# Attention by units of two heads, its scaling on GpSimd, weight tiles released before evictions, and Gram products that alternate heads

## What is computed

```
def causal_block_attention(q, k, v, scale):      # 8 heads, q and k 96 wide, v 64 wide
    for blk in range(S // Q_BLOCK):              # 8 blocks of 128 queries
        s = jnp.einsum('bqhd,bkhd->bhqk', qb, k[:, :kend]) * scale
        s = jnp.where(mask, s, -1e30)
        prob = jax.nn.softmax(s, axis=-1)
        outs.append(jnp.einsum('bhqk,bkhd->bqhd', prob, v[:, :kend]))
```

## Time and profile before

| | us |
|---|---|
| median of three runs | 4064.01 (4061.86 to 4067.34) |
| the profiled run | 4065.56 |
| its span | 4064.3 |
| granted TensorE clock, mean | 0.949 of full |
| TensorE busy | 3753.2, 92% of the span |
| VectorE, ScalarE, GpSimd busy | 1815.3, 1317.5, 1172.0 |

### The profile page before, as it was taken

One profiled execution on the slowest core, in us unless ns is written; L12 is line 12 of the kernel. 1 busy time (PEld: TensorE's weight loads), 2 busy tenths in 40 slices (PEclk: granted clock), 3 DMA queues, 4 the chain that ended last, 5 costly groups with the idle time before them and its releaser, 6 DMA issues.

```text
span 4064.3 us, 44734 instructions
## 1 busy us (share of the span) xinstructions
PE 3753.2 (92%) x18398; PEld 3094.9 (76%) x18398; DVE 1815.3 (45%) x2380; ACT 1317.5 (32%) x2129; POOL 1172.0 (29%) x624
## 2 busy tenths in 40 slices
PE   5998998979799987999999898999987989999998
PEld 4786877878777766888888767777666868888886
DVE  3435444444155534233233353887543444444435
ACT  3323132222344323221221343776123233232323
POOL 3322313231100232333333211576133313222321
PEclk8988898988999999999999999999999999999999
DMA  4101010000100343111111222222344421111111
GB/s 119 53 1 53 1 46 19 19 29 18 39 12 1 99 144 95 50 50 47 50 49 47 73 88 86 70 86 86 99 154 143 148 80 50 47 48 51 47 47 52
DMA packets 282074, 253.63 MB, mean 62 GB/s; under 512 B 11333, under 2 KB 221569, under 8 KB 281872
## 3 DMA queue, kind: packets, MB, share of 16 engines
q1 hardware_dynamic: 267264, 216.52, 17.7%
q10 hardware_dynamic: 11520, 25.17, 1.6%
q0 software_dynamic: 3088, 9.10, 0.6%
HBM read 214.04 MB, written 36.70 MB: 62 GB/s over the span
## 4 chain that ended last, share of the span: by engine, by line


## 5 line engine op out<-in xcount | busy, mean ns | idle before, releaser
L401 POOL TENSOR_TENSOR weight_lo<-stage,weight_hi 128x1024 fp32r<-128x1024 f32 (+4 forms) x265 | 634.5, 2400 | 1551.9 <-ACT weight_hi L393 1551.7
L364 PE MATMUL psum<-hT_hi,weight_hi 128*128 128x512 f32 x2240 | 895.8, 400 | 13.7 <-ACT sig_g L744 6.6
L365 PE MATMUL psum<-hT_lo,weight_hi 128*128 128x512 f32 x2240 | 882.0, 394 | 0.0
L366 PE MATMUL psum<-hT_hi,weight_lo 128*128 128x512 f32 x2240 | 881.3, 393 | 0.0
L364 PEld LDWEIGHTS psum<-hT_hi,weight_hi 128*128 128x128 f32 x2240 | 427.9, 191 | 112.3 <-issue 16.0
L365 PEld LDWEIGHTS psum<-hT_lo,weight_hi 128*128 128x128 f32 x2240 | 427.2, 191 | 93.8 <-issue 6.1
L366 PEld LDWEIGHTS psum<-hT_hi,weight_lo 128*128 128x128 f32 x2240 | 426.3, 190 | 89.8
L393 ACT ACTIVATE weight_hi<-stage 128x1024 fp32r<-128x1024 f32 (+4 forms) x329 | 313.5, 974 | 462.2 <-PE psum L366 381.7
L1935 DVE TENSOR_TENSOR x<-x,psum 128x512 f32<-128x512 f32 x432 | 290.1, 686 | 216.4 <-PE psum L366 215.8
L364 PE MATMUL psum<-weight_hi,act_hi 128*128 128x512 f32 x864 | 339.9, 393 | 0.0
L366 PE MATMUL psum<-weight_hi,act_lo 128*128 128x512 f32 x864 | 339.4, 393 | 0.0
(11 more groups left out here) (371 smaller groups left out, 6045.9 us busy)
## 6 DMA issues: line engine op xcount, KB each, us to landing
stage<-in_w_in SPq DMA_DIRECT2D x64, 512.0 KB, 4.0
stage<-in_w_up SPq DMA_DIRECT2D x44, 512.0 KB, 3.9
scratch_gates<-gate ACTq DMA_DIRECT2D x64, 256.0 KB, 2.0
gs<-scratch_gates SPq DMA_DIRECT2D x64, 256.0 KB, 2.8
stage<-in_w_out SPq DMA_DIRECT2D x32, 512.0 KB, 4.8
stage<-in_w_ffn_up SPq DMA_DIRECT2D x32, 512.0 KB, 4.0
stage<-in_w_ffn_down SPq DMA_DIRECT2D x32, 512.0 KB, 3.9
stage<-in_w_down SPq DMA_DIRECT2D x22, 512.0 KB, 3.4
```

Of the source, the lines that this page charges most:

```text
L364: q.matmul(out, stat[0], mov[0], start=first, stop=False)
L365: q.matmul(out, stat[0], mov[1], start=False, stop=False)
L366: return q.matmul(out, stat[1], mov[0], start=False, stop=final)
L401: g.q.tensor_tensor(lo, K.staged(w), hi.bitcast(F32), ALU.subtract).then_inc(*S.w_lo_pool.up(w))
```

## The change

**Attention.** A unit is a block of queries of both heads of a pair: 32 units, a lag of one unit between steps where it was two for the transposes. The scores of head h use banks 2h and 2h+1 (2h alone for narrow units); P and PT have four buffers each, two heads of two units. After a unit's two exponents VectorE takes both reciprocals (`dve_exponent`), and GpSimd multiplies each P in place by them (`pool_exponent`, 64 instructions, widths 128 to 1024); only then does TensorE transpose. Three banks, 4 to 6, take the transposes and the fed steps. The output product has `vh` stationary (64 columns) and PT moving (128 columns), the two heads in turn to partitions 0 to 63 and 64 to 127 of bank 7, so that the result is oT itself: ScalarE writes oT_hi (32 of 128x128, L1617), VectorE oT_lo. `otok`, its 64 evictions, 32 transposes and 16 evictions go. The next pair's steps are fed two at a time, from the third of a pair's eight iterations.

**Releases.** In the merges, the compression and the feed-forward's last group, `released` stands between TensorE's last product and the eviction of its result.

**Gram.** A step has two quads of a batch, the two heads of one chunk, which alternate product by product. The two batches in flight take turns by such a step; before they took turns quad by quad.

```diff
-        elif ring == "work":
-            banks = (3 + self.ring_at["work"] % 4,)
-            self.ring_at["work"] += 1
+        elif ring == "turned":
+            banks = (4 + self.ring_at["turned"] % 3,)
+            self.ring_at["turned"] += 1
...
-def pe_gram(K, blk, n, side, q):
-    pe, (_, c, h) = K.pe, quads(n)[q]
-    b = K.open(("gram", blk, n, q))
+def pe_gram(K, blk, n, side, i):
+    pe, c = K.pe, 2 * n + i
+    b = [K.open(("gram", blk, n, 2 * i + h)) for h in range(2)]
     pe.wait_ge(K.S.act_evac, ("tok", blk, 3, 4))
-    rhs = K.AR[hd(h), c, :, :]
-    pe.q.matmul(b[:, 0:2 * P], K.Bt[hd(h), c, :], rhs, start=True, stop=True)
-    pe.q.matmul(b[:, 2 * P:4 * P], K.Kt[hd(h), c, :], rhs, start=True, stop=True).then_inc(*K.S.mm.up(("gram", blk, n, q)))
-def dve_gram(K, blk, n, side, q):
+    for o, left in ((0, K.Bt), (2 * P, K.Kt)):
+        for h in range(2):
+            mm = pe.q.matmul(b[h][:, o:o + 2 * P], left[hd(h), c, :], K.AR[hd(h), c, :, :], start=True, stop=True)
+            if o:
+                mm.then_inc(*K.S.mm.up(("gram", blk, n, 2 * i + h)))
+def dve_gram(K, blk, n, side, i):
     v, S = K.v, K.S
-    v.wait_ge(S.mm, ("gram", blk, n, q))
-    if n >= 2:
-        v.wait_ge(S.mm, ("Y", blk, n - 2, 3))
-    v.q.tensor_tensor(K.m4[side][:, q, :], K.bank(("gram", blk, n, q)), K.mask4[:, :], ALU.mult).then_inc(*S.dve_evac.up(("gram", blk, n, q)))
-    K.free(("gram", blk, n, q), S.dve_evac)
+    for q in (2 * i, 2 * i + 1):
+        v.wait_ge(S.mm, ("gram", blk, n, q))
+        if n >= 2:
+            v.wait_ge(S.mm, ("Y", blk, n - 2, 3))
+        v.q.tensor_tensor(K.m4[side][:, q, :], K.bank(("gram", blk, n, q)), K.mask4[:, :], ALU.mult).then_inc(*S.dve_evac.up(("gram", blk, n, q)))
+        K.free(("gram", blk, n, q), S.dve_evac)
...
-TURN_LAG, OUT_LAG = 2, 1
-UNITS = [(pair, h, qb) for pair in range(HEADS // 2) for h in range(2) for qb in QB_ORDER]
+TURN_LAG, OUT_LAG = 1, 1
+UNITS = [(pair, qb) for pair in range(HEADS // 2) for qb in QB_ORDER]
...
-def unit_banks(u):
-    return (2,) if UNITS[u][2] < 4 else (0, 1)
+def score_banks(u, h):
+    return (2 * h,) if UNITS[u][1] < 4 else (2 * h, 2 * h + 1)
+def unit_rows(K, u, h):
+    return K.Pm[2 * (u % 2) + h], K.PT[2 * (u % 2) + h]
...
 def act_exponent(K, u):
-    a, S, (pair, h, qb) = K.a, K.S, UNITS[u]
+    a, S, (pair, qb) = K.a, K.S, UNITS[u]
     n = (qb + 1) * P
-    a.wait_ge(S.dve_op, ("max", u))
-    if u >= len(K.Pm):
-        a.wait_ge(S.mm, ("PT", u - len(K.Pm)))
-    a.q.activation(K.Pm[u % len(K.Pm)][:, 0:n], K.bank(("score", u))[:, 0:n], ACT.Exp, bias=K.st[:, 1, u:u + 1], scale=SCALE,
-                   accum_out=K.st[:, 2, u:u + 1]).then_inc(*S.act_evac.up(("exp", u)))
-    K.free(("score", u), S.act_evac)
+    for h in range(2):
+        c = 2 * u + h
+        a.wait_ge(S.dve_op, ("max", u, h))
+        if u >= 2:
+            a.wait_ge(S.mm, ("PT", u - 2, h))
+        a.q.activation(unit_rows(K, u, h)[0][:, 0:n], K.bank(("score", u, h))[:, 0:n], ACT.Exp, bias=K.st[:, 1, c:c + 1],
+                       scale=SCALE, accum_out=K.st[:, 2, c:c + 1]).then_inc(*S.act_evac.up(("exp", u, h)))
+        K.free(("score", u, h), S.act_evac)
+def dve_exponent(K, u):
+    v, S, (pair, qb) = K.v, K.S, UNITS[u]
+    n = (qb + 1) * P
+    for h in range(2):
+        c = 2 * u + h
+        v.wait_ge(S.act_evac, ("exp", u, h))
+        v.q.reciprocal(K.st[:, 3, c:c + 1], K.st[:, 2, c:c + 1]).then_inc(*S.dve_op.up(("1/sum", u, h)))
+def pool_exponent(K, u):
+    g, S, (pair, qb) = K.g, K.S, UNITS[u]
+    n = (qb + 1) * P
+    for h in range(2):
+        c, rows = 2 * u + h, unit_rows(K, u, h)[0]
+        g.wait_ge(S.dve_op, ("1/sum", u, h))
+        g.q.tensor_scalar(rows[:, 0:n], rows[:, 0:n], K.st[:, 3, c:c + 1], None, ALU.mult).then_inc(*S.pool_op.up(("P", u, h)))
 def pe_turn_p(K, u):
-    pe, S, (pair, h, qb) = K.pe, K.S, UNITS[u]
-    for j0 in range(0, qb + 1, 4):
-        nj = min(4, qb + 1 - j0)
-        b = K.open(("PT", u, j0), "work")
-        pe.wait_ge(S.act_evac, ("exp", u))
-        for j in range(nj):
-            mm = pe.q.transpose(b[:, j * P:(j + 1) * P], K.Pm[u % len(K.Pm)][:, (j0 + j) * P:(j0 + j + 1) * P], K.ident[:, :])
-        mm.then_inc(*S.mm.up(("PT", u, j0)))
-    S.mm.at[("PT", u)] = S.mm.n
...
 def pe_output(K, u):
-    pe, S, (pair, h, qb) = K.pe, K.S, UNITS[u]
+    pe, S, (pair, qb) = K.pe, K.S, UNITS[u]
     b = K.open(("o", u), (7,))
-    pe.wait_ge(S.act_evac, ("PT", u, 0))
+    pe.wait_ge(S.act_evac, ("PT", u, 1, 0))
     if qb >= 4:
-        pe.wait_ge(S.dve_evac, ("PT", u, 4))
+        pe.wait_ge(S.dve_evac, ("PT", u, 1, 4))
     for j in range(qb + 1):
-        mm = pe.q.matmul(b[:, 0:VDIM], K.PT[u % len(K.PT)][:, j, :], K.vh[pair % 2][:, j, h, :], start=j == 0, stop=j == qb)
+        for h in range(2):
+            mm = pe.q.matmul(b[hd(h), 0:P], K.vh[pair % 2][:, j, h, :], unit_rows(K, u, h)[1][:, j, :], start=j == 0, stop=j == qb)
     mm.then_inc(*S.mm.up(("o", u)))
+def act_output(K, u):
+    a, S, (pair, qb) = K.a, K.S, UNITS[u]
+    a.wait_ge(S.mm, ("o", u))
+    a.q.activation(K.oT[0][:, pair, qb * P:(qb + 1) * P], K.bank(("o", u))[:, 0:P], ACT.Copy).then_inc(*S.br_hi.up(("oT", u)))
 def dve_output(K, u):
-    v, S, (pair, h, qb) = K.v, K.S, UNITS[u]
-    v.wait_ge(S.mm, ("o", u))
-    v.wait_ge(S.dve_op, ("1/sum", u))
-    if pair:
-        v.wait_ge(S.mm, ("oT", pair - 1, 4))
-    v.q.tensor_scalar(K.otok[:, qb, h * VDIM:(h + 1) * VDIM], K.bank(("o", u))[:, 0:VDIM], K.st[:, 3, u:u + 1], None,
-                      ALU.mult).then_inc(*S.dve_evac.up(("o", u)))
-    K.free(("o", u), S.dve_evac)
...
-    for q in range(4):
-        o.do("gram", blk, n, side, q)
+    for i in range(2):
+        o.do("gram", blk, n, side, i)
         yield
...
         w0 = o.take(tiles)
         for t in range(NT):
             o.do("compress", part, t, w0)
-        o.released(tiles)
+            if t == NT - 1:
+                o.released(tiles)
+            o.do("compressed", part, t)
...
     for i in range(len(UNITS) + TURN_LAG + OUT_LAG):
         if i < len(UNITS):
             pair = UNITS[i][0]
-            if i % (2 * NT) == 0:
+            if i % NT == 0:
                 finish(feed)
-                feed = order_pair(o, pair + 1, "work") if pair + 1 < HEADS // 2 else iter(())
-                fed = -3
+                feed = order_pair(o, pair + 1, "turned") if pair + 1 < HEADS // 2 else iter(())
+                fed = -2
             o.do("score", i)
         fed += 1
-        more = 1 if fed > 0 else 0
+        more = 2 if fed > 0 else 0
         advance(feed, more)
         if 0 <= i - TURN_LAG < len(UNITS):
             o.do("turn_p", i - TURN_LAG)
         advance(feed, more)
-        u = i - TURN_LAG - OUT_LAG
-        if u >= 0:
-            o.do("output", u)
-            if u % (2 * NT) == 2 * NT - 1:
-                for t0 in range(0, NT, 4):
-                    o.do("pair_out", UNITS[u][0], t0)
+        if i - TURN_LAG - OUT_LAG >= 0:
+            o.do("output", i - TURN_LAG - OUT_LAG)
         advance(feed, more)
         if i < len(UNITS):
             o.do("exponent", i)
...
             for t in range(tokens):
-                o.do("merge_out", m, part, t, n, w0, pre[t])
+                o.do("merge_out", m, part, t, n, w0)
                 if t == tokens - 1:
                     o.released(4)
+                o.do("merge_rows", m, part, t, n, pre[t])
```

146 lines of the change are left out of this document (74 added, 72 removed).

## The result

| | before | changed |
|---|---|---|
| median, us | 4065.58 (4 runs, 4061.86 to 4067.34) | 4088.59 (4 runs, 4084.6 to 4089.28) |
| ratio to before | | 1.0056, 95% interval 1.0038 to 1.0073 |
| span of the profiled run | 4064.3 | 4083.3 |
| attention, first score to first product with oT_hi | 1124.5 to 1368.7: 244.1 | 1103.0 to 1417.8: 314.8 |
| from there to the end | 2695.6 | 2665.5 |

The change makes the kernel slower by 0.56%, where I had forecast 0.34% faster. The time is 1.6 us above my range (4028 to 4087), and the direction was wrong too. The profiled run is the fastest of the four, 4084.6, so the traces differ by 19 us and the medians by 23. Three things moved, and the spans tell them apart: everything ahead of attention is 21.5 us shorter, attention 70.7 us longer, everything behind it 30.1 us shorter.

What follows compares the result with a forecast made beforehand. TensorE, busy 92% of the span, was taken as the bound, its instruction stream in attention and waits for weights or norms in the merges. Attention +15, releases -24, Gram -5 made -14 against 4065.56: 4051.6, forecast 4050 us, range 4028 to 4087.

Steps and rivals of the forecast that it cites:

- What is removed: Attention: cheaper output products and no transposes of otok take 31 us of TensorE's work off the stage.
- The sum: Whole kernel: attention +15, releases -24 and Gram products -5 make -14 us, so 4051.6.
- The exponent behind the output, 12.3 us a pair: Attention: scores wait for exponents queued on ScalarE behind an older unit's output, leaving TensorE idle 12.3 us a pair.
- The sum with VectorE's price: Attention: if GpSimd's multiplication cost what VectorE's row shows, 754 ns, the stage would change by +12 us.
- GpSimd's price: Attention: GpSimd's multiplication of 1024 columns taken as 1.18 us, half its two-tensor row, bounded by 754 and 2358 ns.
- Rival (a): Attention: GpSimd costs what its two-tensor row says; stage +33, sum +4, kernel 4068; chance 0.16.
- Rival (b), the clock: Attention: TensorE's clock falls to half after waits over 2.8 us; +38 on the forecast, 4088; chance 0.17.
- Releases, -24: Merges, compression, feed-forward: weight splits ahead of evictions shorten TensorE's waits by 19 and lost clock by 5.
- 3114.60: TensorE's 12.59 us wait at that time, nearly all load time of the first weights; claimed to shrink by 1.5.
- the compression, where I had +2: Compression: the last eviction now stands behind a split that waits for its load, costing 2 us.
- Gram products, -5: Gram products: GpSimd's first level needs the sixth masked copy, not the seventh; -0.6 us for each of 8 waits, -5.
- the wait at L975: TensorE's wait behind GpSimd's first level after the Gram products, 8 times, 31.1 us in all; claimed to fall to 3.3 each.

Runs made afterwards that it cites:

- f7: The changed kernel with P's scaling on VectorE and the exponent between the copies of PT and the output; 4007.11 us, ratio to before 0.9857.
- f1: The changed kernel with the scaling of P on VectorE in place of GpSimd; 4039.76 us, ratio to before 0.9942.
- f3: The changed kernel with the exponent's step ahead of the output but behind the copies of PT; 4045.34 us, ratio to before 0.9956.
- f5: The changed kernel with the exponent's step right behind the scores; 4044.77 us, ratio to before 0.9956.
- f8: The changed kernel with GpSimd's scaling as a product of two tensors, the second the broadcast reciprocal; 4046.84 us, ratio to before 0.9954.
- g1: The changed kernel with another form of GpSimd's instruction in each pair, pairs 1 and 2 not normalised; 4053.02 us in one run.
- e4: The kernel before with the earlier releases and the new Gram order, without the attention part; 4014.98 us, ratio to before 0.9884.

## Why the prediction was wrong

Step by step, as it was put:

- **What is removed** (31 us of TensorE, 0.06 us a record of the new product): right. Idle time taken off, the output's products fill 63.7 us of the stage before and 37.1 in f7, and the transposes of `otok`, 3.6, are gone: 30.2 us. But the stage's other products, the same in number, take 9 us longer in f7 than before (0.132 us a transpose of P for 0.121, for instance), in f1 14 us. The sum took their work over unchanged.
- **The exponent behind the output, 12.3 us a pair:** the mechanism was right (f3, f5), the size too large: 31.9 us of waits in the stage, not 49. With the scaling on VectorE the place in the order is worth 32.0 us (f1 against f7).
- **The sum with VectorE's price:** f1's 260.6 us against 257 looks like a confirmation, but two errors cancel in it. TensorE is busy 211.3 us where I had 189.5 in the pairs and idle for 49 where I had 67.
- **GpSimd's price:** this is the step that failed, and with it the clock, which the sum put at nothing. "I take half of the first, 1.18 us, since it streams one tensor in place of two": it takes 2.84. Both bounds were rows of another form or another engine, and the number lay outside them, above. Rival (a) with +33 was too small for the same reason; f8, whose form at 1.89 us lies inside the bounds, gives 271.0, +27 on before. An estimate from my own two figures, +15 at 1.18 us and +33 at 2.36, carried on to 2.84, is +40; the stage has +70.7. The 30 us that are left are about the 31 by which TensorE's busy time exceeds f1's, at a clock of 0.85 for 0.96.
- **Rival (b), the clock:** right that it falls, incomplete in its condition. I had it decide "from the first wait over 2.8 us". The one wait of 2.83 us in the first pair was followed by the half clock, but so were shorter ones: in the last pair it fell behind 1.47 and 0.61 us, as a third wait of 1.55 began. Since (a) and (b) have one cause here, they came together, and I had added neither to the other: +70.7 is more than (a), and (b) on top. That (b)'s own time, 4088, is the measured one is luck: it has 53 us more for the stage in place of 70.7, and 29 less for the two small parts in place of some 44. And my range ended at 4087, below the time of a rival to which I gave 0.17.
- **The rule of the Trainium skill** ("GPSIMD Engine Reference", section 4.1, one-input operations roughly at line rate): the copy in g1 comes near to it (1.04 us for 1024 columns), tensor and scalar doesn't (2.84 us against VectorE's 0.75), and the measurement decides.
- **Releases, -24:** -29.3. Right in the merges (0.85 + 4.12, 2.83, 3.9, 4.2 and 2.85 gone; their two stretches are 25.2 us shorter, where my terms, with the clock, make 26); wrong at 3114.60 (0 in place of -1.5), and in the compression, where I had +2 and the waits fell from 14.75 to 11.69 and from 5.05 to 3.25, the stretch by 3.1. I had the last eviction pay for the split ahead of it; nothing that TensorE waits for shows such a cost. That the split brought its low part and the next load forward is my reading.
- **Gram products, -5:** -14.3. The 0.6 us a batch was 0.86 at full clock, and 2.0 to 2.4 where the clock is at half, which four of the eight batches are. I had written "more where the clock is at half" and given it no number, and the 3 to 5.5 us between the fourth and the fifth batch were in no term. That GpSimd starts one masked copy earlier was right. That the wait at L975 shrinks to 3.3 us a time was wrong: it is 4.2, since the alternating products also end earlier.
- **The sum:** -43.6 for the two small parts (-47.7 by e4) where I had -29, +68 for attention where I had +15.

## What to carry to other kernels

Before work is moved to an engine, its price there is to be had for that very form of instruction; where no row shows it, rows of other forms are no bounds, and the range has to hold the dearer case together with what it drags along. When TensorE gets faster or waits in short pieces, its clock is part of the price: two terms that have one cause (a slow helper, a fallen clock) add up instead of being alternatives. And an exponent, or any step that frees a bank that the next product needs, belongs ahead of whatever its engine does for an older unit: here that one place in the order was worth 45 us with the scaling on GpSimd and 32 with it on VectorE.

## What the runs showed of the hardware that I had not expected

- GpSimd, 1024 f32 columns in place: copy 1.04 us, product of a tensor with a broadcast one 1.89, tensor times a scalar per partition 2.84, tensor times a constant 2.77. VectorE does the same multiplication in 0.75.
- TensorE's granted clock fell to half behind waits of 1.47 and 0.61 us with short work between, as a wait of 1.55 began. Over the stage it was 0.85, and 0.96 when products that nobody needs filled a part of the waits.
- Products with 64 stationary and 128 moving columns take 0.06 us a record (two records each) when neighbours go to different halves of PSUM's partitions; in runs to the same half 0.09.
